# Stick-breaking attention: the logarithms as two fp32r halves for the triangle product

## The chip, the cores and the metric

The kernel runs on one core of a Trainium2 chip. The core has TensorE (matmul), VectorE, ScalarE, GpSimd and SyncE, each with its own instruction stream; streams meet only at semaphores. The metric is the device time of one execution in microseconds, as the median of several runs. "Rest", "values" and the other names of steps below are this document's.

## The reference

One inference step of a two-layer encoder for 512 prompt tokens and 64 sample tokens. Each layer has two feed-forward parts, a mixer with four branches, and a per-layer embedding. The change lies in the fourth branch, stick-breaking attention, with 4 heads of 64:

```python
z = jnp.einsum('bqhd,bkhd->bhqk', q, k).astype(jnp.float32) * (HEAD_DIM ** -0.5)
mask = k_pos[None, :] < q_pos[:, None]
log_beta = jax.nn.log_sigmoid(z)
log_1mb = jnp.where(mask, jax.nn.log_sigmoid(-z), 0.0)
rest = lax.cumsum(log_1mb, axis=3, reverse=True) - log_1mb
a = jnp.where(mask, jnp.exp(log_beta + rest), 0.0)
return jnp.einsum('bhqk,bkhd->bqhd', a.astype(v.dtype), v)
```

A key's weight depends on a sum of logarithms over all later keys up to the query. The kernel computes sp = log(1 + exp(z)), which is minus log_1mb, and z minus the sum of sp over the key itself and the later ones.

## The kernel before

All values are held transposed, features or keys on the 128 partitions and tokens along the free axis. Weights are split into a high part `whi` and a low part `wlo`, and activations into `u_hi` and `u_lo`, all of type fp32r; `products` (L587) multiplies three combinations of them in matmuls of 288 columns. GpSimd makes `wlo` (L1906), ScalarE `whi` (L554). The instruction order on each engine is written out by hand, and the stages follow each other.

The stick-breaking stage of a layer goes through 21 steps, listed in `SB` (L1417). For each of the 4 heads of the prompt there are four blocks of 128 keys, from the last block to the first. A block has the queries from its own position on, so it is 128, 256, 384 and 512 columns wide in this order. Then come five steps for the sample tokens, 256 columns each (4 heads by 64 queries): the 64 new keys and four blocks of cached keys. All prompt steps and the first sample step are diagonal: part of the block is masked.

A step i does this:

- TensorE, `sb_logits` (L1462, L1471): keys by queries, fp32, into PSUM bank 4 or 5.
- ScalarE (L1556 to L1558): absolute value, exp, log, into `sq`.
- VectorE (L1608): `spx` = max(z, 0) + that logarithm, and in a diagonal step the mask (L1576, L1575). The last of them raises `sb_sp`.
- TensorE, `sb_rest` (L1482): the triangle of minus ones `trineg` times `spx`, fp32, added to the logits in PSUM. In all but a head's first block L1486 adds minus the sum of the earlier blocks, kept in `sqsum`.
- VectorE, `finish` (L1584 to L1600): minimum with 0 into `arg`, the new `sqsum` (L1590, L1594, L1595), and after ScalarE's exp (L1563) the mask of `arg`.
- TensorE, `sb_values` (L1500, L1506): values by `arg`, into another bank.

TensorE's order in iteration i is logits(i), rest(i-1), values(i-2), and a quarter of one gate projection in fp32r (12 matmuls of L587, in the iterations 0 to 19). VectorE's order is finish(i-1), then spx(i). ScalarE does absolute value, exp and log of i, then the exp of i-1; after every fourth step it also copies the gate out of PSUM and rounds the next weight, after which GpSimd splits that weight.

Of the kernel before, what the change touches and what calls it, by code (L numbers as in the profile page):

```python
# [25 lines left out]
F32R = mybir.dt.float32r  # L26
ALU = mybir.AluOpType
# [5 lines left out]
T = SEQ + DEC  # L33
# [13 lines left out]
TB = (T + 127) // 128  # L47
# [6 lines left out]
F_, Q_, V_, G_, CA_, CB_, SQ_, SK_, SV_, BQ_, BK_, BV_ = 0, 2, 4, 6, 8, 10, 12, 14, 15, 16, 18, 20  # L54
NPROJ = 22
# [33 lines left out]
def trunk(nc, a, o):  # L89
# [3 lines left out]
    with ExitStack() as ctx:  # L93
        base = nc.sbuf_base
        arena = ctx.enter_context(nc.sbuf_tensor("arena", [128, (nc.sbuf_usable_end - base) // 4 - 16], F32))
        limit = nc.sbuf_usable_end
# [20 lines left out]
        keep = Region((base + 31) // 32 * 32)  # L117
# [6 lines left out]
        headones = keep("headones", [128])  # L124
        trineg = keep("trineg", [128])
        negones = keep("negones", [128])
        later = keep("later", [128])
        eye64 = keep("eye64", [CHUNK])
        lvmask = keep("lvmask", [6, CHUNK // 2])
# [40 lines left out]
        proj_at = rm.at  # L170
# [35 lines left out]
        sbtok = rb("sbtok", [TB, 512])  # L206
        spx = rb("spx", [2, 512])
        arg = rb("arg", [2, 512])


        gkeep = proj
# [29 lines left out]
        ps = ctx.enter_context(nc.psum_tensor("ps", [128, 8, 512], F32))  # L241
# [90 lines left out]
        sb_tok = sem("sb_tok")  # L332
# [3 lines left out]
        sb_sp = sem("sb_sp")  # L336
# [143 lines left out]
        def bounds_vector(dve):  # L480

            n = [0]

            def link(ins):
                n[0] += 1
                ins.then_inc(lb_step, 1)
                dve.wait_ge(lb_step, n[0])

            lg, mx, sm = lb_work[:, 0:4], lb_work[:, 4:6], lb_work[:, 6:8]
            link(dve.tensor_tensor(mx, lg[:, 0:2], lg[:, 2:4], ALU.max))  # L490
            link(dve.tensor_tensor(lg[:, 0:2], lg[:, 0:2], mx, ALU.subtract))
            link(dve.tensor_tensor(lg[:, 2:4], lg[:, 2:4], mx, ALU.subtract))
            for g in range(2):
                half = slice(64 * g, 64 * g + 64)
                link(dve.tensor_copy(sinkcol[half], sinks_all[half, :, :, g]))
            dve.wait_ge(lb_exp, 1)
            link(dve.tensor_tensor(sm, lg[:, 0:2], lg[:, 2:4], ALU.add))
            link(dve.reciprocal(sm, sm))
            link(dve.tensor_tensor(lg[:, 0:2], lg[:, 0:2], sm, ALU.mult))
            link(dve.tensor_tensor(lg[:, 2:4], lg[:, 2:4], sm, ALU.mult))  # L500
            link(dve.tensor_tensor(lb_all[:, 0, :], lg[:, 0:2], lg[:, 0:2], ALU.subtract))
            link(dve.tensor_tensor(lb_all[:, 1, :], lg[:, 0:2], lg[:, 2:4], ALU.add))
            link(dve.tensor_tensor(lb_all[:, 1, :], lb_all[:, 1, :], lg[:, 0:2], ALU.subtract))
            link(dve.tensor_scalar(lb1m[:], lb_all[:], -1.0, 1.0, ALU.mult, ALU.add))

        def setup_scalar(act):
            for n, name in enumerate(GAIN_NAMES):
# [16 lines left out]
        def layer(L):  # L524
# [6 lines left out]
            def before(s):  # L531

                return L * IN_LAYER[s]
# [226 lines left out]
            def link(dve, ins):  # L760

                steps[0] += 1
                ins.then_inc(dve_step, 1)
                dve.wait_ge(dve_step, steps[0])
# [661 lines left out]
            def sb_first(i):  # L1426
                return i == 0 or SB[i][0] != SB[i - 1][0]

            def sb_diagonal(i):

                hd, kb = SB[i]
                return hd is not None or kb is None
# [44 lines left out]
            def sb_rest(pe, i):  # L1477

                nk, w = sb_shape(i)
                bk = 4 + i % 2  # L1480
                pe.wait_ge(sb_sp, i + 1 + before(sb_sp))
                ins = pe.matmul(ps[0:nk, bk, 0:w], trineg[0:nk, 0:nk], spx[0:nk, i % 2, 0:w], start=False, stop=sb_first(i), skip_group_check=True)  # L1482
                if not sb_first(i):
                    q0, z0 = (0, 0) if SB[i][0] is None else (128 * SB[i][1] + 128, 128)
                    pe.wait_ge(sb_sum, sb_sums(i - 1) + before(sb_sum))
                    ins = pe.matmul(ps[:, bk, z0:w], negones[:], sqsum[:, q0:q0 + w - z0], start=False, stop=True, skip_group_check=True)  # L1486
                ins.then_inc(sb_arg, 1)
# [80 lines left out]
            def dve_sb(dve):  # L1568
                lk = lambda ins: link(dve, ins)

                def mask(i, x):

                    if SB[i][0] is None:
                        v = x[0:64, i % 2, 0:256].rearrange("p (h q) -> p h q", h=4)
                        return dve.tensor_tensor(v, v, later[0:64, 0:64].unsqueeze(1).to_broadcast([64, 4, 64]), ALU.mult)  # L1575
                    return dve.tensor_tensor(x[:, i % 2, 0:128], x[:, i % 2, 0:128], later[:], ALU.mult)  # L1576

                def finish(i):
                    hd, kb = SB[i]
                    nk, w = sb_shape(i)  # L1580
                    dve.wait_ge(sb_arg, i + 1 + before(sb_arg))
                    if i >= 2:
                        dve.wait_ge(sb_pv, i - 1 + before(sb_pv))
                    dve.tensor_scalar(arg[0:nk, i % 2, 0:w], ps[0:nk, 4 + i % 2, 0:w], 0.0, None, ALU.min).then_inc(sb_min, 1)  # L1584

                    if kb != 0:
                        if hd is None:
                            if kb is None:
                                lk(dve.memset(sqsum[:, 0:w], 0.0))
                            ins = dve.tensor_tensor(sqsum[0:nk, 0:w], sqsum[0:nk, 0:w], spx[0:nk, i % 2, 0:w], ALU.add)  # L1590
                        else:
                            q0 = 128 * kb
                            if not sb_first(i):
                                lk(dve.tensor_tensor(sqsum[:, q0 + 128:SEQ], sqsum[:, q0 + 128:SEQ], spx[:, i % 2, 128:w], ALU.add))  # L1594
                            ins = dve.tensor_copy(sqsum[:, q0:q0 + 128], spx[:, i % 2, 0:128])  # L1595
                        ins.then_inc(sb_sum, 1)
                        dve.wait_ge(sb_sum, sb_sums(i) + before(sb_sum))
                    if sb_diagonal(i):
                        dve.wait_ge(sb_exp, i + 1 + before(sb_exp))
                        mask(i, arg).then_inc(sb_a, 1)  # L1600

                for i in range(len(SB)):
                    nk, w = sb_shape(i)
                    z = ps[0:nk, 4 + i % 2, 0:w]
                    if i:
                        finish(i - 1)
                    dve.wait_ge(sb_ln, i + 1 + before(sb_ln))
                    ins = dve.scalar_tensor_tensor(out=spx[0:nk, i % 2, 0:w], in0=z, scalar=0.0, in1=sq[0:nk, i % 2, 0:w], op0=ALU.max, op1=ALU.add)  # L1608
                    if sb_diagonal(i):
                        lk(ins)  # L1610
                        ins = mask(i, spx)
                    ins.then_inc(sb_sp, 1)
                finish(len(SB) - 1)


# [480 lines left out]
```

## Time and profile before

| | us |
|---|---|
| median of 3 runs (3318.54 to 3319.71) | 3318.58 |
| the profiled execution | 3317.39 |
| its span, first to last instruction | 3315.7 |
| TensorE busy, 24147 matmuls | 3166.0 (95%) |
| VectorE busy | 1217.3 (37%) |
| ScalarE busy | 1101.5 (33%) |
| GpSimd busy | 1215.8 (37%) |
| share of TensorE in the chain that ended last | 87% |
| L1482, rest of the triangle: 32 records of 256 columns | 11.2, 431 ns each |
| stick-breaking stage, layer 0: first logits to last values | 788.0 to 880.9 |

The span is the time between the first and the last instruction; the execution's own time is 1.7 us more. An fp32 matmul leaves two records in the trace, an fp32r matmul one. The ends of matmuls are modelled, so a matmul's place is better read from its start and the start of the next one. "PEld" rows are weight loads.

### The profile page before, as it was taken

The numbers are of one execution on the slowest core, as the hardware profiler recorded it, in microseconds if no ns is written. First come the engines' busy times: TensorE is split into PE (matmuls) and PEld (weight loads), VectorE is DVE, ScalarE is ACT, GpSimd is POOL, SyncE is SP. The second block draws the span as 40 slices with busy tenths as digits, with TensorE's granted clock in tenths as the row PEclk, the third lists the DMA queues.
The fourth block names the chain that finished last, engine by engine and source line by source line (L and its number), as shares of the span: only waits on it lengthen the run. The fifth ranks groups of instructions, "written<-read, shape, count | busy, mean of one in ns | idle before, by whom it ended". The sixth has DMA issues, their size and how long they took to land.

```text
span 3315.7 us, 56545 instructions
## 1 busy us (share of the span) xinstructions
PE 3166.0 (95%) x24147; PEld 3037.2 (92%) x24147; DVE 1217.3 (37%) x1452; ACT 1101.5 (33%) x1528; POOL 1215.8 (37%) x564
## 2 busy tenths in 40 slices
PE   8999999899999999999989999998999999999998
PEld 7999989896799899999889999898867998999997
DVE  4232134744443423212342321348444434232124
ACT  3333222235433332322333332322354333323232
POOL 5433442231134433344343334423312344333443
PEclk9999999999999999999999999999999999999999
DMA  3222312221122122222112222122211221222221
GB/s 101 83 82 79 86 57 68 67 80 47 34 82 76 58 79 86 80 88 75 58 50 77 85 82 83 52 66 73 74 41 45 82 77 58 82 81 85 84 68 42
DMA packets 455951, 236.17 MB, mean 71 GB/s; under 512 B 18630, under 2 KB 454150, under 8 KB 455814
## 3 DMA queue, kind: packets, MB, share of 16 engines
q1 hardware_dynamic: 445792, 227.05, 23.5%
q10 hardware_dynamic: 10022, 7.15, 0.7%
q8 instruction: 104, 1.70, 0.2%
q14 instruction: 33, 0.27, 0.0%
HBM read 228.53 MB, written 5.63 MB: 71 GB/s over the span
## 4 chain that ended last, share of the span: by engine, by line
PE 87%; DVE 7%; ACT 3%; issue 1%; POOL 1%; ACTq 0%; DMA 0%; DVEq 0%; SPq 0%; POOLq 0%
PE ps L587 77%; PE ps L610 2%; PE ps L1482 1%; DVE uf L794 1%; PE ps L1781 1%; PE ps L620 1%; DVE sqsum L774 1%; PE ps L1500 1%; PE ps L1462 1%; DVE u_lo L788 1%; PE ps L604 1%; POOL u_lo L788 1%; DVE kgate L1094 0%; ACT u_hi L712 0%; PE ps L1486 0%
## 5 line engine op out<-in xcount | busy, mean ns | idle before, releaser
L1906 POOL TENSOR_TENSOR wlo<-wraw,whi 128x1024 fp32r<-128x1024 f32 x432 | 1078.3, 2496 | 1936.5 <-ACT whi L554 1936.0
L587 PE MATMUL ps<-u_hi,whi 128*128 128x288 f32 x4800 | 1055.1, 301 | 36.8 <-ACT ybr L1658 11.8
L587 PE MATMUL ps<-u_lo,whi 128*128 128x288 f32 x4800 | 1035.4, 297 | 0.0
L587 PE MATMUL ps<-u_hi,wlo 128*128 128x288 f32 x4800 | 1034.6, 297 | 0.0
L587 PEld LDWEIGHTS ps<-u_hi,whi 128*128 128x128 f32 x4800 | 770.0, 189 | 73.9 <-issue 31.6
L554 ACT ACTIVATE whi<-wraw 128x1024 fp32r<-128x1024 f32 x432 | 457.3, 1059 | 959.7 <-PE ps L587 959.3
L587 PEld LDWEIGHTS ps<-u_lo,whi 128*128 128x128 f32 x4800 | 773.5, 189 | 0.0
L587 PEld LDWEIGHTS ps<-u_hi,wlo 128*128 128x128 f32 x4800 | 773.4, 189 | 0.0
L837 DVE TENSOR_TENSOR sq<-sq,ps 128x576 f32<-128x576 f32 x88 | 66.4, 755 | 750.9 <-PE ps L587 750.9
L587 PE MATMUL ps<-s_hi,whi 128*128 128x288 f32 x1408 | 302.7, 296 | 0.0
L587 PE MATMUL ps<-s_lo,whi 128*128 128x288 f32 x1408 | 302.7, 296 | 0.0
L587 PE MATMUL ps<-s_hi,wlo 128*128 128x288 f32 x1408 | 302.7, 296 | 0.0
L774 DVE TENSOR_TENSOR sqsum<-sqsum,sq 128x576 f32<-128x576 f32 x70 | 102.5, 1465 | 506.7 <-ACT sq L689 505.2
L841 DVE TENSOR_TENSOR s_lo<-sq,s_hi 128x576 f32 x88 | 239.4, 2721 | 10.9
L587 PEld LDWEIGHTS ps<-s_lo,whi 128*128 128x128 f32 x1408 | 225.9, 188 | 0.0
L587 PEld LDWEIGHTS ps<-s_hi,whi 128*128 128x128 f32 x1408 | 225.8, 188 | 0.0
L587 PEld LDWEIGHTS ps<-s_hi,wlo 128*128 128x128 f32 x1408 | 225.5, 188 | 0.0
L1260 DVE SCALAR_TENSOR_TENSOR yc<-zc,taps_all,yc 128x606 f32<-128x606 f32 x120 | 142.6, 1189 | 4.2
L554 ACT ACT_TABLE_LOAD x44 | 56.5, 1283 | 229.7 <-PE ps L587 229.7
L788 POOL TENSOR_TENSOR u_lo<-uf,u_hi 128x576 fp32r<-128x576 f32 x40 | 60.3, 1515 | 80.7 <-ACT u_hi L712 79.8
L587 PE MATMUL ps<-m_split,whi 128*128 128x288 f32 x512 | 89.4, 297 | 0.3 <-DVE m_split L1690 0.3
L803 POOL TENSOR_TENSOR h<-h,uf 128x576 f32<-128x576 f32 x32 | 55.9, 1768 | 67.3 <-DVE uf L811 67.3
(273 smaller groups left out, 2639.0 us busy)
## 6 DMA issues: line engine op xcount, KB each, us to landing
wraw<-in_ffn_up SPq DMA_DIRECT2D x176, 512.0 KB, 3.7
wraw<-in_w_in SPq DMA_DIRECT2D x104, 512.0 KB, 3.7
wraw<-in_ffn_down SPq DMA_DIRECT2D x64, 512.0 KB, 4.0
wraw<-in_ffn_down SPq DMA_DIRECT2D x32, 384.0 KB, 3.3
wraw<-in_w_out SPq DMA_DIRECT2D x16, 512.0 KB, 3.8
wraw<-in_ple_gate_w SPq DMA_DIRECT2D x16, 512.0 KB, 3.9
wraw<-in_w_branch SPq DMA_DIRECT2D x16, 256.0 KB, 2.6
xtok<-in_x_prompt SPq DMA_DIRECT2D x4, 512.0 KB, 6.5
```

Of the source, the lines that this page charges most:

```text
L554: act.activation(whi[:, i % SPLIT, :], wraw[:, i % RAW, :], ACT.Copy).then_inc(w_rounded, 1)
L587: ins = pe.matmul(ps[:, 2 * p + f, 0:HT], wt[:, part, w], x[:, k, HT * f:HT * f + HT], start=start and n == 0 and c == 0, stop=stop and n ...
L604: pe.matmul(ps[:, 1, 0:128], ones[:], ident[:], start=True, stop=True)
L610: ins = pe.matmul(ps[:, 0, SAME * tb:SAME * tb + same], x[:, t0:t0 + 128], ones[:, 0:same], start=start and tb == 0, stop=stop and tb == T ...
L620: pe.matmul(flat(3)[:, 0:SEQ], ones[:], roots[:, 0:SEQ], start=True, stop=True)
L774: dve.tensor_tensor(sqsum[:], sqsum[:], sq[:, k % 2, :], ALU.add).then_inc(sq_added, 1)
L788: engine.tensor_tensor(u_lo[:, k, :], uf[:, k, :], u_hi[:, k, :], ALU.subtract).then_inc(signal, 1)
L803: engine.tensor_tensor(h[:, k, :], h[:, k, :], uf[:, k, :], ALU.add).then_inc(signal, 1)
L837: dve.tensor_tensor(halves(x), halves(x), pair(2 * q + 1), ALU.mult).then_inc(up_mul, 1)
L841: dve.tensor_tensor(s_lo[:, bass.ds(it * 2 + q, 1), :].rearrange("p a n -> p (a n)"), x, s_hi[:, bass.ds(it * 2 + q, 1), :].rearrange("p a ...
L1260: ins = dve.scalar_tensor_tensor(out=yc[:, c, :], in0=zc[:, c, w:w + YW], scalar=wc, in1=yc[:, c, :], op0=ALU.mult, op1=ALU.add)
L1906: pool.tensor_tensor(wlo[:, i % SPLIT, :], wraw[:, i % RAW, :], whi[:, i % SPLIT, :], ALU.subtract).then_inc(w_split, 1)
```

## The change

`spx` is split on VectorE in two halves of type fp32r: `spx_hi` is `spx` rounded, by a multiplication with 1, and `spx_lo` the remainder, by a subtraction. A copy of the triangle of type fp32r is made once. TensorE multiplies the triangle with the high half and then the low half, in place of one fp32 matmul. `sb_sp` is raised by the subtraction. The halves lie where the projected values and the cached keys were, which are no longer read by then. The product with `sqsum`, the logits and the values stay fp32.

```diff
@@ -124,6 +124,7 @@
         negones = keep("negones", [128])
+        trineg_r = keep("trineg_r", [128], F32R)
@@ -206,6 +207,11 @@
         arg = rb("arg", [2, 512])
+
+        rv = Region(proj_at + BV_ * T * 4)
+        spx_hi = rv("spx_hi", [2, 512], F32R)
+        assert rv.at <= proj_at + NPROJ * T * 4
+        spx_lo = Region(limit - 8192 - 32)("spx_lo", [2, 512], F32R)
@@ -502,6 +508,7 @@
             link(dve.tensor_scalar(lb1m[:], lb_all[:], -1.0, 1.0, ALU.mult, ALU.add))
+            link(dve.tensor_copy(trineg_r[:], trineg[:]))
@@ -1479,7 +1486,9 @@
                 pe.wait_ge(sb_sp, i + 1 + before(sb_sp))
-                ins = pe.matmul(ps[0:nk, bk, 0:w], trineg[0:nk, 0:nk], spx[0:nk, i % 2, 0:w], start=False, stop=sb_first(i), skip_group_check=True)
+                for x in (spx_hi, spx_lo):
+                    ins = pe.matmul(ps[0:nk, bk, 0:w], trineg_r[0:nk, 0:nk], x[0:nk, i % 2, 0:w], start=False, stop=sb_first(i) and x is spx_lo,
+                                    skip_group_check=True)
@@ -1606,10 +1615,13 @@
                     ins = dve.scalar_tensor_tensor(out=spx[0:nk, i % 2, 0:w], in0=z, scalar=0.0, in1=sq[0:nk, i % 2, 0:w], op0=ALU.max, op1=ALU.add)
+                    lk(ins)
                     if sb_diagonal(i):
-                        lk(ins)
-                        ins = mask(i, spx)
-                    ins.then_inc(sb_sp, 1)
+                        lk(mask(i, spx))
+                    if i == 0:
+                        dve.wait_ge(sb_tok, TB + 2 + before(sb_tok))
+                    lk(dve.tensor_scalar(spx_hi[0:nk, i % 2, 0:w], spx[0:nk, i % 2, 0:w], 1.0, None, ALU.mult))
+                    dve.tensor_tensor(spx_lo[0:nk, i % 2, 0:w], spx[0:nk, i % 2, 0:w], spx_hi[0:nk, i % 2, 0:w], ALU.subtract).then_inc(sb_sp, 1)
```


On VectorE, where the 512-column block of a head is followed by the next head's first block, before (`later` is the mask, `sb_ln` the wait for ScalarE's logarithm):

```order
L1608 SCALAR_TENSOR_TENSOR spx<-ps,sq 128x512 [waits sb_ln]
L1576 TENSOR_TENSOR spx<-spx,later 128x128 [waits dve_step]
L1584 TENSOR_SCALAR arg<-ps 128x512 [waits sb_pv,sb_arg]
L1576 TENSOR_TENSOR arg<-arg,later 128x128 [waits sb_exp]
L1608 SCALAR_TENSOR_TENSOR spx<-ps,sq 128x128 [waits sb_ln]
L1576 TENSOR_TENSOR spx<-spx,later 128x128 [waits dve_step]
```

And after, from the same place (lines are those of the changed file, 9 higher here):

```order
L1617 SCALAR_TENSOR_TENSOR spx<-ps,sq 128x512 [waits sb_ln]
L1585 TENSOR_TENSOR spx<-spx,later 128x128 [waits dve_step]
L1623 TENSOR_SCALAR spx_hi<-spx 128x512 [waits dve_step]
L1624 TENSOR_TENSOR spx_lo<-spx,spx_hi 128x512 [waits dve_step]
L1593 TENSOR_SCALAR arg<-ps 128x512 [waits sb_pv,sb_arg]
L1585 TENSOR_TENSOR arg<-arg,later 128x128 [waits sb_exp]
L1617 SCALAR_TENSOR_TENSOR spx<-ps,sq 128x128 [waits sb_ln]
L1585 TENSOR_TENSOR spx<-spx,later 128x128 [waits dve_step]
L1623 TENSOR_SCALAR spx_hi<-spx 128x128 [waits dve_step]
L1624 TENSOR_TENSOR spx_lo<-spx,spx_hi 128x128 [waits dve_step]
```

Two operations and their waits stand between the mask and the minimum; the signal for TensorE moved from the mask to the second of them.

On TensorE, the same step before: logits of the next head, rest, values, start of the next gate.

```order
L1462 MATMUL ps<-proj 128x128 [waits sb_min]
L1482 MATMUL ps<-spx,trineg 128x512 [waits sb_sp]
L1486 MATMUL ps<-sqsum,negones 128x384 [waits sb_sum]
L1500 MATMUL ps<-arg,sbtok 64x384 [waits sb_a]
L587 MATMUL ps<-u_hi,whi 128x288 [waits gate_out,w_split]
```

And after:

```order
L1469 MATMUL ps<-proj 128x128 [waits sb_min]
L1490 MATMUL ps<-spx_hi,trineg_r 128x512 [waits sb_sp]
L1490 MATMUL ps<-spx_lo,trineg_r 128x512
L1495 MATMUL ps<-sqsum,negones 128x384 [waits sb_sum]
L1509 MATMUL ps<-arg,sbtok 64x384 [waits sb_a]
L594 MATMUL ps<-u_hi,whi 128x288 [waits gate_out,w_split]
```

One fp32 matmul became two of fp32r; the wait for `sb_sp` stands ahead of the first.

## Rows read from the trace of the kernel before

**Rows 1.** Stretches of layer 0: from:to us, length, engines busy (instructions), granted clock.
```profile
803.00:820.00 17.00, 17.00 (x79) 10.80 (x78) 7.38 (x21) 9.39 (x19) 2.37 (x1) 1.00 0.11 32
...
884.00:886.00 2.00, 2.00 (x10) 2.00 (x10) 2.00 (x4) 2.00 (x4) 0.00 (x0) 0.50 0.00 0
```

**Rows 2.** Timeline, one head: start us, duration us, engine, line, operation, count.
```profile
810.81 0.29 DVE L1576 TENSOR_TENSOR spx<-spx,later 128x128 f32<-128x128 f32 x1
...
812.44 0.70 PE L1482 MATMUL ps<-spx,trineg 128*128 128x256 f32 x2
...
815.44 0.29 DVE L1576 TENSOR_TENSOR spx<-spx,later 128x128 f32<-128x128 f32 x1
...
815.45 1.12 PE L1462 MATMUL ps<-proj 64*128 64x512 f32 x2
...
816.50 0.91 PE L1482 MATMUL ps<-spx,trineg 128*128 128x384 f32 x2
...
817.25 0.59 PE L1486 MATMUL ps<-sqsum,negones 128*128 128x256 f32 x2
...
820.07 0.29 DVE L1576 TENSOR_TENSOR spx<-spx,later 128x128 f32<-128x128 f32 x1
...
820.57 1.13 PE L1482 MATMUL ps<-spx,trineg 128*128 128x512 f32 x2
...
821.53 0.81 PE L1486 MATMUL ps<-sqsum,negones 128*128 128x384 f32 x2
...
823.77 0.69 DVE L1576 TENSOR_TENSOR arg<-arg,later 128x128 f32<-128x128 f32 x1 [0.70 <-ACT arg L1563]
...
824.69 0.29 DVE L1576 TENSOR_TENSOR spx<-spx,later 128x128 f32<-128x128 f32 x1
...
825.47 0.49 PE L1482 MATMUL ps<-spx,trineg 128*128 128x128 f32 x2
...
825.88 1.07 PE L1500 MATMUL ps<-arg,sbtok 128*64 128x512 f32 x2
```

**Rows 3.** Timeline, fp32r matmuls of a gate part, TensorE.
```profile
814.56 0.43 PE L587 MATMUL ps<-u_hi,whi 128*128 128x288 f32 x2
...
814.82 0.43 PE L587 MATMUL ps<-u_lo,whi 128*128 128x288 f32 x2
```

**Rows 4.** Groups by line and shape, VectorE: busy us, mean ns, idle before.
```profile
L1594 DVE TENSOR_TENSOR sqsum<-sqsum,spx 128x256 f32<-128x256 f32 x8 | 3.3, 416 | 0.0
...
L1690 DVE TENSOR_TENSOR m_split<-msum,m_split 128x576 fp32r<-128x576 f32 x16 | 12.1, 758 | 0.5
...
L839 DVE TENSOR_SCALAR s_hi<-sq 128x576 f32 x88 | 40.8, 464 | 13.4 <-DVE sq L837 5.7
```

**Rows 5.** Timeline, first two steps of the stage, layer 0.
```profile
792.51 0.49 PE L1482 MATMUL ps<-spx,trineg 128*128 128x128 f32 x2 [1.60 <-DVE spx L1576]
...
794.44 0.29 DVE L1576 TENSOR_TENSOR spx<-spx,later 128x128 f32<-128x128 f32 x1
...
795.36 0.70 PE L1482 MATMUL ps<-spx,trineg 128*128 128x256 f32 x2
```

**Rows 6.** Timeline, last steps of the stage, layer 0.
```profile
876.01 1.60 DVE L1590 TENSOR_TENSOR sqsum<-sqsum,spx 128x256 f32<-128x256 f32 x1
...
877.65 0.42 DVE L1608 SCALAR_TENSOR_TENSOR spx<-ps,sq 128x256 f32<-128x256 f32 x1
...
878.13 0.70 PE L1482 MATMUL ps<-spx,trineg 128*128 128x256 f32 x2 [2.12 <-DVE spx L1608]
```

**Rows 7.** Timeline, where the sample group begins and one of its steps.
```profile
854.32 0.94 PE L1471 MATMUL ps<-proj 64*64 64x64 f32 x8
...
855.20 1.12 PE L1482 MATMUL ps<-spx,trineg 128*128 128x512 f32 x2
...
863.00 0.41 DVE L1608 SCALAR_TENSOR_TENSOR spx<-ps,sq 128x256 f32<-128x256 f32 x1
...
865.45 0.70 PE L1482 MATMUL ps<-spx,trineg 128*128 128x256 f32 x2
```

## The prediction, made before the changed kernel ran

> **What bounds the kernel now.** I read the table of stretches first, for the stage that the change touches: in a 17 us stretch of the stick-breaking stage TensorE is busy for all 17.00 us, VectorE for 7.38 [rows 1]. So TensorE looks like the bound and VectorE idle. Its matmul ends are modelled, though, so I went on to the timeline of one head, in order of time. I call the four pieces of a step i on TensorE logits (L1462, L1471), rest (L1482 and, after a head's first block, L1486), values (L1500, L1506) and gates (L587). rest(i) comes one step after logits(i), and it needs spx(i), VectorE's last product before it. The reader is to compare, for each rest, the end of VectorE's mask L1576 with the start of L1482 [rows 2]. From that end to TensorE's start the signal takes 0.06 us, as the one true wait shows (spx ends at 878.07, the rest starts at 878.13) [rows 6]. Then the slack of a step is:
> - 256 columns: ready 811.10, started 812.44, slack 1.28 us.
> - 384 columns: ready 815.73, started 816.50, slack 0.71.
> - 512 columns: ready 820.36, started 820.57, slack 0.15.
> - 128 columns: ready 824.98, started 825.47, slack 0.43.
>
> TensorE is the bound in the steady part, but with VectorE only 0.15 to 1.28 us behind it. TensorE waits for VectorE at two places of a layer: 1.60 us at the first rest [rows 5] and 2.12 us at the last [rows 6]. Both layers show the same pattern. What comes after the stage starts from its end, so what the stage gains or loses shifts the end of the kernel.
>
> **What the change takes off TensorE.** An fp32 rest of 384 columns takes 0.75 us to the next weight load (816.50 to 817.25), one of 512 takes 0.96 (820.57 to 821.53) [rows 2]: 1.64 ns a column and 0.12 fixed, four columns' time at 2.4 GHz. The fp32r matmuls of L587 follow each other at 0.26 us for two of 288 columns [rows 3]: 0.13 each, one column's time. Two such matmuls of w columns and the same fixed part make 0.56 us at 512, so 0.40 saved, 0.30 at 384, 0.20 at 256. At 128 the block is a head's first, its rest took 0.41 (825.47 to 825.88) [rows 2], and with weight loads that no longer hide well I count 0.10. A head saves 1.0 us. The sample group has five rests of 256 columns, 0.2 each. Bounds: nothing saved, if a switch between fp32 and fp32r costs what the passes give, and 1.07 a head, if exactly half of the four passes goes.
>
> **What it puts on VectorE, and on the path.** Each of the 21 steps of a layer gets two operations between the mask and the signal. The low half is a subtraction of two SBUF tensors: L1594 takes 0.416 us at 256 columns, L1690 0.758 at 576, with an fp32r result [rows 4]: 0.28, 0.42, 0.55 and 0.68 us for 128, 256, 384 and 512. The high half is the same operation as L839, 0.464 us at 576 [rows 4]; with about 0.15 fixed, like the subtraction, that is 0.22, 0.29, 0.36 and 0.43. Each waits for the one before through a semaphore, 0.03 us. Together 0.56, 0.77, 0.97 and 1.17 us. The upper bound for the high half is the subtraction's rate, 0.25 more at 512. Behind the signal VectorE's next operation is the minimum of the step, which waits for the rest anyway; behind the waiting L1482 on TensorE are L1486, values, gates and the next logits, so a late rest moves everything.
>
> Steady part, step by step, against the slacks above:
> - 256: 0.77 against 1.28, hidden; TensorE then is 0.2 early.
> - 384: 0.97 against 0.71 less 0.2, so TensorE waits 0.46. The rest is 0.3 shorter, TensorE is 0.16 late.
> - 512: slack 0.15 and 0.16; VectorE's chain runs through the minimum of the step before and is some 0.1 later (estimate). 1.17 + 0.1 - 0.31 = 0.96 of waiting; 0.4 shorter rest leaves 0.56.
> - 128: 0.56 against 0.43, 0.13 late by that count. But VectorE's mask L1576 at 823.77 took 0.69 us where others take 0.29, and now starts later, behind what held it. I take 0.
>
> A head: 0.46 + 0.96 - 1.0 = +0.42 us, four heads +1.68. The first head has more: its first rest already waited for VectorE, so 0.56 is added in full. In its second step the slack was 795.36 - 794.73 - 0.06 = 0.57 [rows 5]; VectorE is 0.56 later and TensorE 0.46, so 0.77 against 0.47, 0.30 late. Together +0.86. In the fourth head the logits that follow are the sample group's, 0.88 us up to the rest (854.32 to 855.20) where a head's first logits take about 0.42 [rows 7]; that hides 0.45 more. Sample group: spx is ready at 863.41, its rest starts at 865.45 [rows 7], so 0.77 is hidden and four rests save 0.8. The last rest waits for VectorE: +0.77 - 0.2 = +0.57. A layer: 1.68 + 0.86 - 0.45 - 0.8 + 0.57 = +1.86 us, two layers +3.7. The copy of the triangle to fp32r is one small VectorE operation in the first layer before its first wait for TensorE, where VectorE idles for microseconds: nothing. More semaphores and the shifted addresses: nothing.
>
> The profiled execution took 3317.4 us, 1.7 outside its span; the median of the runs shown is 1.2 above it. The difference is carried over to the median: 3318.6 + 3.7 = 3322.3.
>
> **The clock.** The granted clock is 1.00 in the stage and 0.50, the lower level of 1.2 GHz, from 884 to 886, with TensorE busy all the time [rows 1]; before that lay the wait of 2.12 us and the hand-over to the next stage. Here it costs while dense matmuls run. The change adds about 0.6 us of idle time before that place and moves it by 1.9 us, so more or less of the slow stretch can fall on dense matmuls: between -1.5 and +3.4 us a layer, of which I take 0. The Trainium skill ("TensorE: Matmul & The Clock Gate", HAM oscillation — how this bites in real kernels) says that idle gaps on TensorE bring the clock down and that it has to be earned again, which speaks against a change that adds waits. The trace agrees for the gap at the end of the stage; no row shows a fall from waits of about 1 us inside the stage, and by that rule alone the sum would be higher.
>
> **Rivals.**
> 1. *TensorE's gain wins.* If VectorE's two operations overlapped what is there (the mask's tail, slacks larger than the rows say), only the saving would count: 4 x 1.0 + 5 x 0.2 = 5 us a layer, 3308.6. For it: TensorE busy 17.00 of 17. Against it: slacks of 0.15 and 0.43 us, and a chain of semaphores that allows no overlap. The faster outcome also needs the first and last waits not to grow.
> 2. *VectorE becomes the bound outright.* The high half runs at the subtraction's rate (0.07 to 0.25 more a step) and the switches eat half of the saving. Per head the two late steps then cost 0.45 more and the saving is 0.5 less, the step of 128 comes 0.2 late: +1.1 a head. With 0.1 for the first steps and 0.4 more for five sample rests: +5 a layer, 10 in all, so 3332. It decides as soon as the two operations take over 1.3 us at 512 columns or the rest saves under 0.2. For it: the slack is gone at 512 even in the forecast. Against: L839 is the same kind of operation, to the same type, at 0.464.
> 3. *A slow clock after the stage.* The longer last wait lets the slow stretch fall on dense matmuls of the next stage: up to 3.4 us a layer beyond the forecast, 3325 to 3329.
> 4. *GpSimd holds up the new subtractions.* L1590, two SBUF inputs, took 1.60 us at 876.01 instead of about 0.42 [rows 6] while GpSimd split a weight. One such hit on a late step costs 1 to 2 us, four a layer 4 to 8. GpSimd's run comes at the same place in each head, so it would be all or none; the split of 512 starts well before it.
>
> **How the numbers follow.** About 0.2% (6.6 us) is what a measurement of this kernel can tell from no change. Forecast, +1 to +6.5 us: 0.60. Rival 1 in full or in part, below +1: 0.12, of which 0.05 lies beyond -6.6. Rivals 2, 3 and 4, above +6.5 us: 0.12, 0.08 and 0.05, and 0.03 for what I don't see. The range takes in both bounds of the two unknown costs and a slow stretch: 3316 to 3330. Faster by over 0.2% 0.05, within 0.2% 0.67, slower by over 0.2% 0.28.
>
> **What would show it.** Per head the stage lasts 17.5 us instead of 17.1; L1482's successors wait for the low half in the steps of 384 and 512 columns (about 0.5 and 1 us) and not in those of 256 and 128 after the first head; the last wait is some 0.8 us longer; two fp32r matmuls of 512 columns lie within 0.56 us of each other's successor. The high half at 0.43 us and the low at 0.68 for 512 columns. If rests of 384 and 512 start without a wait, or the high half takes 0.68, or an fp32r rest of 512 columns takes more than 0.75 us, the forecast's steps are wrong. So is its sum, if the time between the two stick-breaking stages changes.

## The result, and the profile after

| | before | after |
|---|---|---|
| median, 4 runs each (us) | 3318.56 (3317.40 to 3319.71) | 3341.64 (3340.34 to 3342.85) |
| profiled execution, its span (us) | 3317.39, 3315.7 | 3342.85, 3341.1 |
| mean granted clock of TensorE | 0.982 | 0.975 |
| stage, first logits to last values, layers 0 and 1 (us) | 92.97, 92.97 | 98.43, 95.54 |

The changed kernel is slower: ratio 1.0069 [1.0057, 1.0081], 23 us, where 3.7 were forecast and 3330 was the top of the range. The page of the changed kernel, its span, the busy time by engine and the shares of the chain that ended last:

```profile
span 3341.1 us, 56632 instructions
...
PE 3179.9 (95%) x24147; PEld 3052.8 (91%) x24147; DVE 1251.5 (37%) x1537; ACT 1101.9 (33%) x1528; POOL 1213.3 (36%) x564
...
PE 85%; DVE 9%; ACT 3%; issue 1%; POOL 1%; ACTq 0%; DMA 0%; DVEq 0%; SPq 0%; POOLq 0%
```

TensorE has as many records as before and is busy 14 us more, although the edit takes work off it. That is the first hint that its work ran slower somewhere. A head of the stage looks as forecast. The timeline of a head, the steps of 384 and 512 columns and the next head's first block (to be set against [rows 2]):

```profile
821.18 0.36 DVE L1623 TENSOR_SCALAR spx_hi<-spx 128x384 fp32r<-128x384 f32 x1
821.57 0.56 DVE L1624 TENSOR_TENSOR spx_lo<-spx,spx_hi 128x384 fp32r<-128x384 f32 x1
...
822.19 0.44 PE L1490 MATMUL ps<-spx_hi,trineg_r 128*128 128x384 f32 x1 [0.42 <-DVE spx_lo L1624]
...
822.64 0.59 PE L1495 MATMUL ps<-sqsum,negones 128*128 128x256 f32 x2
...
825.76 0.43 DVE L1623 TENSOR_SCALAR spx_hi<-spx 128x512 fp32r<-128x512 f32 x1
826.22 0.69 DVE L1624 TENSOR_TENSOR spx_lo<-spx,spx_hi 128x512 fp32r<-128x512 f32 x1
...
826.96 0.50 PE L1490 MATMUL ps<-spx_hi,trineg_r 128*128 128x512 f32 x1 [0.94 <-DVE spx_lo L1624]
...
827.54 0.81 PE L1495 MATMUL ps<-sqsum,negones 128*128 128x384 f32 x2
...
831.48 0.33 PE L1490 MATMUL ps<-spx_hi,trineg_r 128*128 128x128 f32 x1
```

TensorE now waits for the low half, 0.42 us at 384 columns and 0.94 at 512, and the rest of 512 columns takes 0.58 us to the next product (826.96 to 827.54) instead of 0.96. The first and the last rest of the stage, with the logits behind the first (to be set against [rows 5, 6]):

```profile
794.50 0.33 PE L1490 MATMUL ps<-spx_hi,trineg_r 128*128 128x128 f32 x1 [2.18 <-DVE spx_lo L1624]
...
796.85 1.65 PE L1469 MATMUL ps<-proj 64*128 64x384 f32 x2
...
884.60 0.47 PE L1490 MATMUL ps<-spx_hi,trineg_r 128*128 128x256 f32 x1 [3.10 <-DVE spx_lo L1624]
```

The second of these rows lasts 1.65 us, far over what its column count asks (512 columns take 1.12 in [rows 2]). A stretch right there has the granted clock at 0.50, the lower level of 1.2 GHz; before, it was at 1.00 from 743.5 to 880.0 us, of which [rows 1] show a part. The columns of such stretches are, from here on: from:to, length, busy us (count) of PE, PEld, DVE, ACT, POOL, granted clock, DMA share, GB/s.

```profile
797.00:799.00 2.00, 2.00 (x4) 0.92 (x5) 0.43 (x1) 0.46 (x1) 0.00 (x0) 0.50 0.00 0
```

Setting the two traces side by side, place by place, gives the lag of the changed kernel (start time after minus start time before):

| place | before, us | lag, us |
|---|---|---|
| stage of layer 0 begins | 788.0 | +1.4 |
| stage of layer 0 ends | 881.0 | +6.9 |
| token sums of the second feed-forward part's norm | 1109.7 | +8.5 |
| token sums ahead of the per-layer embedding | 1574.9 | +6.8 |
| feed-forward sums, layer 1 | 2118.8 | +13.6 |
| stage of layer 1 begins, ends | 2433.2, 2526.2 | +14.4, +16.9 |
| second feed-forward part's norm, layer 1 | 2755.0 | +18.7 |
| token sums ahead of the per-layer embedding, layer 1 | 3218.7 | +18.6 |
| end | 3315.7 | +25.4 |

The lag grows in the stages (5.5 and 2.6 us) and by 5 to 7 us each across the token sums ahead of the per-layer embedding, code that the change does not touch. These sums are 40 fp32 matmuls, 80 records in the trace. The stationary operand of each, the one that is loaded as weights, is a block of squares, and the moving one is 64 equal columns of ones, so that each sum is written 64 times over (L610, now L617). Before, the timeline row of the group and a stretch inside it:

```profile
1574.89 9.14 PE L610 MATMUL ps<-ones,sq 128*128 128x64 f32 x80 [0.74 <-ACT e L1806]
```
```profile
1575.00:1580.00 5.00, 5.00 (x46) 5.00 (x46) 0.00 (x0) 3.17 (x5) 2.35 (x1) 1.00 0.09 28
```

And after:

```profile
1581.73 14.86 PE L617 MATMUL ps<-ones,sq 128*128 128x64 f32 x80 [0.74 <-ACT e L1818]
```
```profile
1585.00:1590.00 5.00, 5.00 (x26) 5.00 (x25) 0.00 (x0) 1.37 (x2) 0.05 (x1) 0.50 0.38 105
1590.00:1595.00 5.00, 5.00 (x25) 5.00 (x25) 0.00 (x0) 1.37 (x2) 0.00 (x0) 0.50 0.01 3
```

The same 80 records take 14.86 us instead of 9.14, at a granted clock of 0.50 instead of 1.00: 26 records in 5 us instead of 46, TensorE busy all the time in both. The wait ahead of them is 0.74 us in both. Summed over the kernel, the stretches at 0.50 come to about 120 us before and 168 after. So the 23 us are, roughly, 8 in the two stages (2.6 each, and 2.9 more where the clock fell early in layer 0) and 11 or 12 in two groups of sums. Another 1.6 and 1.8 come between a stage's end and the next norm's sums, where the stretch at 0.50 lasts 10.2 us instead of 6.8 (880.0 to 886.8 before, 884.8 to 895.0 after, in layer 0).

### The profile page after: what moved, and what is told of

Its sections match the earlier page's. It is cut to its first block, busy times and chain, and to the rows that moved or that the text cites. A ratio compares the mean times of both kernels' runs of the same rounds, so it can differ in the third digit from the quotient of the medians.

```text
span 3341.1 us, 56632 instructions
## 1 busy us (share of the span) xinstructions
PE 3179.9 (95%) x24147; PEld 3052.8 (91%) x24147; DVE 1251.5 (37%) x1537; ACT 1101.9 (33%) x1528; POOL 1213.3 (36%) x564
## 4 chain that ended last, share of the span: by engine, by line
PE 85%; DVE 9%; ACT 3%; issue 1%; POOL 1%; ACTq 0%; DMA 0%; DVEq 0%; SPq 0%; POOLq 0%
PE ps L594 75%; PE ps L617 2%; DVE uf L801 1%; PE ps L627 1%; PE ps L1793 1%; DVE sqsum L781 1%; PE ps L611 1%; DVE u_lo L795 1%; PE ps L1490 1%; POOL u_lo L795 1%; DVE kgate L1101 0%; PE ps L1509 0%; DVE roots L1145 0%; ACT u_hi L719 0%; DVE roots L786 0%
## 5 line engine op out<-in xcount | busy, mean ns | idle before, releaser
L611 PE MATMUL ps<-ident,ones 128*128 128x128 f32 x528 | 84.7, 324 | 1.6 <-DVE lb_work L483 1.6
```

Of the source, the lines that this page charges most:

```text
L611: pe.matmul(ps[:, 1, 0:128], ones[:], ident[:], start=True, stop=True)
```

## The experiments

Two theories stood against each other. P: the stage costs 2 to 3 us a layer, and the rest comes from when later work is reached, since the clock is granted or not at another place. W: the time is the work and the waits that the change adds. Each kernel was timed beside the kernel before in three rounds; ratios are to that. "Spare matmuls" are fp32 products of `ones` and `ident`, 128 columns, into a PSUM bank that is free there; nobody reads the result. The kernel before has such matmuls of its own around its norms (`keep_clock`, L604).

**shift_before** is the kernel before, without the split, with 12 spare matmuls behind each stage.

```diff
+                for _ in range(12):
+                    pe.matmul(ps[:, 3, 0:128], ones[:], ident[:], start=True, stop=True)
```

> The kernel before with nothing of the change, but 12 more fp32 matmuls of 128 columns on TensorE at the end of each stick-breaking stage (0.21 us each, 2.6 us a layer, no idle time added). Theory P (place in time: most of the 23 us comes from stretches at the lower clock, mainly in the normalisation ahead of the per-layer embedding, which appear or not depending on when that place is reached): the total does not rise by the 5.1 us of added work but differs from that by over 3 us, and the difference sits in stretches at clock 0.50 outside the stick-breaking stages. Theory W (work: the change's own instructions cost it all, wherever they are): 3318.6 + 5.1 = 3323.7, within 1.5 us, and the other stages as long as before.

3326.84 us (3325.52 to 3327.75), ratio 1.0023 [1.0014, 1.0033]: 7.5 us for 5.1 of added work. In layer 0 the sums are long here too, in layer 1 not:

```profile
1573.72 14.95 PE L610 MATMUL ps<-ones,sq 128*128 128x64 f32 x80 [0.74 <-ACT e L1808]
```

So spare work alone, without the change, brought slow sums about. It did so without a delay: they are reached at 1573.72 us, 1.2 earlier than before, since the stretch at 0.50 behind the stage is 3.4 us long instead of 6.8. The total says less: it departs from the 5.1 us of added work by 2.4, under the 3 that theory P expected, and the interval (4.6 to 11 us) holds 5.1 as well.

**shift_after** is the changed kernel with 8 spare matmuls behind each stage, 1.7 us a layer.

> The changed kernel with 8 more fp32 matmuls of 128 columns on TensorE at the end of each stick-breaking stage (1.7 us a layer). Theory P: the total changes by something other than +3.4 us, down as well as up; if the normalisation ahead of the per-layer embedding escapes the lower clock in one layer, about 5 us come back, 3341.6 + 3.4 - 5 = 3340 or less. Theory W: 3345.0 within 1.5 us.

3326.12 us (3325.05 to 3328.14), ratio 1.0021 [1.0011, 1.0031]. The changed kernel with 3.4 us of useless work added is 15.5 us faster than without. The row of the sums and a stretch in them:

```profile
1578.47 9.14 PE L617 MATMUL ps<-ones,sq 128*128 128x64 f32 x80 [0.74 <-ACT e L1820]
```
```profile
1583.00:1588.00 5.00, 5.00 (x47) 5.00 (x47) 0.00 (x0) 2.32 (x4) 0.00 (x0) 1.00 0.35 105
```

Both groups of sums are short again, at a clock of 1.00, though both stages now have the fall inside them (98.43 and 98.36 us). More work took less time, as P has it and W cannot. The two groups of sums give back 11.5 us. A smaller part lies right behind the stages: the stretch at 0.50 there lasts 6.8 us in both layers instead of 10.2. The spare matmuls stand where TensorE was partly idle, so their effect is more than a delay: the sums of layer 0 are reached 3.3 us earlier than in the changed kernel.

**dve_only** makes both halves on VectorE but leaves the rest an fp32 product with the unsplit `spx`.

```diff
-                for x in (spx_hi, spx_lo):
-                    ins = pe.matmul(ps[0:nk, bk, 0:w], trineg_r[0:nk, 0:nk], x[0:nk, i % 2, 0:w], start=False, stop=sb_first(i) and x is spx_lo,
-                                    skip_group_check=True)
+                ins = pe.matmul(ps[0:nk, bk, 0:w], trineg[0:nk, 0:nk], spx[0:nk, i % 2, 0:w], start=False, stop=sb_first(i), skip_group_check=True)
```

> Only VectorE's part of the change: both halves are made and the signal comes after the low half, but TensorE multiplies the unsplit spx in one fp32 matmul as before. By the slacks, a head then costs 0.26 + 0.02 us at 384 columns and about 1.0 to 1.2 us at 512, 0 to 0.1 at 128, so a head's period is 18.3 to 18.5 us instead of 17.1 (the changed kernel: 17.64), and the stage 6 to 8 us longer than before. Theory P expects the total beside that to move by several us in either direction at clock 0.50; theory W expects 3318.6 + 12 to 16 = 3331 to 3335 and no difference elsewhere.

3347.07 us (3337.83 to 3349.05), ratio 1.0077 [1.0060, 1.0094]. A head takes 18.38 us, 1.3 more than before and 0.74 more than after; the stages take 99.98 us. The waits in one head:

```profile
825.03 1.13 PE L1489 MATMUL ps<-spx,trineg 128*128 128x512 f32 x2 [0.93 <-DVE spx_lo L1622]
...
838.34 0.91 PE L1489 MATMUL ps<-spx,trineg 128*128 128x384 f32 x2 [0.22 <-DVE spx_lo L1622]
```

VectorE's two operations alone cost a head what was expected (a period of 18.3 to 18.5 us). The total is 12 us above the upper end of theory W. The sums are long again in both layers.

**pe_only** makes `spx` itself fp32r and lets both matmuls read it, so no halves are made: the low half is left out and the high one counted twice. The main lines, against the changed kernel:

```diff
-        spx = rb("spx", [2, 512])
+        spx = rb("spx", [2, 512], F32R)
...
-                for x in (spx_hi, spx_lo):
+                for n_, x in enumerate((spx, spx)):
...
-                    lk(dve.tensor_scalar(spx_hi[0:nk, i % 2, 0:w], spx[0:nk, i % 2, 0:w], 1.0, None, ALU.mult))
-                    dve.tensor_tensor(spx_lo[0:nk, i % 2, 0:w], spx[0:nk, i % 2, 0:w], spx_hi[0:nk, i % 2, 0:w], ALU.subtract).then_inc(sb_sp, 1)
...
+                    ins.then_inc(sb_sp, 1)
```

> Only TensorE's part: spx is written by VectorE's existing operations as fp32r, no high and low half are made, and both fp32r matmuls read the same tile (so the low half is left out of the computation and the high half counted twice). No step waits for VectorE longer than before, so a head is 1.0 us shorter (period 16.1 us) and the stage about 4.5 to 5 us shorter. Theory W: 3318.6 - 9 to 10 = 3309. Theory P: the stage gains the same, but the total departs from 3309 by over 3 us, at clock 0.50 outside the stage.

3324.49 us (3313.62 to 3325.96), ratio 1.0013 [1.0003, 1.0023]. A head takes 16.29 us (822.73 to 839.02 in the rows) and the stages 89.2, 3.75 less than before in each layer, where 4.5 to 5 were expected. The rest of 512 columns starts 0.06 us behind the end of VectorE's mask, so it waits for VectorE even here, by a little (0.58 us from the logits to it, 0.42 before):

```profile
822.73 0.70 PE L1469 MATMUL ps<-proj 64*128 64x256 f32 x2
...
834.55 0.48 PE L1469 MATMUL ps<-proj 64*128 64x128 f32 x2
...
834.78 0.29 DVE L1585 TENSOR_TENSOR spx<-spx,later 128x128 fp32r<-128x128 f32 x1
...
835.13 0.73 PE L1490 MATMUL ps<-spx,trineg_r 128*128 128x512 f32 x2
835.70 0.81 PE L1495 MATMUL ps<-sqsum,negones 128*128 128x384 f32 x2
...
839.02 0.70 PE L1469 MATMUL ps<-proj 64*128 64x256 f32 x2
...
1569.67 14.99 PE L617 MATMUL ps<-ones,sq 128*128 128x64 f32 x80 [0.74 <-ACT e L1815]
```

The stages are 7.5 us shorter together, and the kernel is slower than before. The last row says why: the sums are reached at 1569.67 and run slowly (in layer 1 too). Rival 1's saving is real at 0.8 us a head, and was lost to the clock. One of this kernel's ten runs took 3313.62, with a mean granted clock of 0.980 where the others had 0.976 or 0.977.

**The sums at 96 columns.** The number of equal columns of ones, `SAME`, is free. Made 96 instead of 64, it adds TensorE columns to these sums and changes nothing else. Two kernels, the changed one and the one before, have this edit:

```diff
-            SAME = 64
+            SAME = 96
```

> The changed kernel, but the token sums of the normalisations of h (80 matmul records each, 6 such places) use 96 instead of 64 columns of the ones; a record takes 0.11 us there either way if the weight load is what paces it. Theory P (the clock falls in the sums ahead of the per-layer embedding at some arrival times because TensorE does too little in them): at full clock each place still takes 9 us, the two that took 14.5 us take 9, and the total falls by 10 us or more, to 3331 or less. Theory W: the sums take longer or as long, nothing else moves, 3341.6 or more.

3326.78 us (3325.34 to 3327.87), ratio 1.0021 [1.0012, 1.0031], 14.9 us less than the changed kernel.

```profile
1579.61 9.17 PE L617 MATMUL ps<-ones,sq 128*128 128x96 f32 x80 [0.74 <-ACT e L1818]
```

> The kernel before with the same 96 columns. Its sums already ran at the full clock. Theory P: no long fall appears, 3318.6 within 4 us, and the changed kernel with 96 columns stands 5 to 8 us above it, which is what the two stages cost by themselves. Theory W: the difference between the two stays 23 us.

3317.48 us (3315.78 to 3319.44), ratio 0.9998 [0.9988, 1.0007]. The kernel before, whose sums were short, gains nothing. A record of 96 columns takes the 0.11 us of one of 64, so no work was saved: what went away is the slow stretch. With it gone from both, the change costs 9.3 us, more than the 5 to 8 expected, of which 7.9 lie in the stages (98.42 and 95.36 against 92.96 and 92.97).

A rival is that the 96 columns only moved the arrival (1579.61 instead of 1581.73). The kept traces speak against it, if the arrival is counted from the end of the last stretch at 0.50 ahead of the sums:

```profile
1564.00:1567.00 3.00, 2.75 (x8) 1.54 (x7) 1.01 (x2) 0.11 (x1) 0.00 (x0) 0.50 0.38 114
...
1568.00:1584.00 16.00, 14.96 (x114) 14.51 (x113) 9.13 (x12) 8.82 (x13) 11.22 (x6) 1.00 0.12 34
```

These two are of the changed kernel, whose stretch at 0.50 ends at 1567.4 us, 14.3 ahead of its sums. The kernels with 64 columns have twelve such groups. Seven began 14.32 to 14.63 us behind that end, and all seven were long; the fall came 2.4 to 2.8 us after their first matmul. Five began 12.22 to 14.23 us behind it, and all five were short. Of the sixteen groups with 96 columns four began 14.32 to 14.48 us behind it, where every group of 64 was long, and all were short. The border is narrow (14.23 against 14.32) and was found in the traces afterwards; no run was made to test it.

**sums96_after_shift** adds the 8 spare matmuls a layer of shift_after to sums96_after.

> The changed kernel with 96 columns and with the 8 extra matmuls at the end of each stage (3.4 us) that took 15.5 us off the changed kernel. Theory P: with the sums out of the clock's reach the arrival time matters little, and this costs what it adds: sums96_after plus 3.4, within 3 us. If the 96 columns have no part in it, this run is again about 15 us faster than sums96_after.

3326.22 us (3324.74 to 3328.20), ratio 1.0021 [1.0012, 1.0031], 0.6 below sums96_after. The spare work that took 15.5 us off now takes off next to nothing, so most of its effect had gone through the sums. But its 3.4 us of work do not show either (3327.2 to 3333.2 was expected), and the stage of layer 1 has its clock fall again (98.35 against 95.36). What pays for both lies behind the stages: from a stage's end to the next norm's sums this kernel takes 2.1 and 2.4 us less than sums96_after although 1.7 us of work stand in between, and the stretch at 0.50 there is 6.8 us long instead of 10.2.

**sums96_values_first** is sums96_after with something for TensorE to do while the low half is made: values(i-2) goes ahead of rest(i-1).

```diff
-                    if 0 <= i - 1 < len(SB):
-                        sb_rest(pe, i - 1)
                     if i >= 2:
                         sb_values(pe, i - 2)
+                    if 0 <= i - 1 < len(SB):
+                        sb_rest(pe, i - 1)
```

> The changed kernel with 96 columns, and with the values of step i-2 ahead of the rest of step i-1 on TensorE. The values (0.31 to 1.0 us) need nothing that is late there, so they fill the waits of 0.42 us at 384 and 0.94 us at 512 columns. A head's period falls from 17.64 to 16.4 to 16.8 us, the stage from 95.5 to 91 to 93 us, the total to 6 to 9 us below sums96_after. If VectorE's chain paces the steps instead (the rest delayed by the values delays the minimum, and that the next spx), the period stays at 17.4 us or more.

3323.73 us (3322.03 to 3324.76), ratio 1.0009 [0.9998, 1.0019]. A head takes 16.50 us instead of 17.64, the stages 91.30 and 94.23, but only 3.05 us less arrive at the end, where 6 to 9 were expected. The wait at 384 columns is gone, the one at 512 stays:

```profile
834.27 0.44 PE L1490 MATMUL ps<-spx_hi,trineg_r 128*128 128x384 f32 x1
...
836.83 0.48 PE L1469 MATMUL ps<-proj 64*128 64x128 f32 x2
837.25 0.86 PE L1509 MATMUL ps<-arg,sbtok 128*64 128x384 f32 x2
...
839.03 0.50 PE L1490 MATMUL ps<-spx_hi,trineg_r 128*128 128x512 f32 x1 [0.93 <-DVE spx_lo L1624]
```

Where the gain went, in two stretches at the end of the stage and behind it:

```profile
874.00:880.00 6.00, 2.83 (x20) 1.92 (x20) 3.17 (x6) 0.98 (x3) 1.33 (x1) 0.56 0.29 89
880.00:886.00 6.00, 3.30 (x17) 3.14 (x16) 4.66 (x7) 4.97 (x9) 0.00 (x0) 0.50 0.00 0
```

TensorE was busy for less than half of the six microseconds ahead of 880, and a stretch at 0.50 of 13.7 us (874.7 to 888.4) lay there in each layer.

**Cover for the idle places.** The last four kernels all have the sums at 96 columns and put spare matmuls where TensorE waited. The three numbers given for each are those ahead of the first rest, ahead of the last rest, and behind the stage. The lines that place them:

```diff
+                        spare(pe, {0: 9, len(SB) - 1: 13}.get(i - 1, 0))
                         sb_rest(pe, i - 1)
                     pe_gate_part(pe, GATES_SW, 2 * KD, i, QUARTERS)
+                spare(pe, 12)
```

**busy_values_first** is sums96_values_first with this (9, 13, 12).

> sums96_values_first with 34 spare fp32 matmuls of 128 columns a layer where TensorE sits idle: 9 ahead of the first rest, 13 ahead of the last, 12 behind the stage, while the next stage's inputs are made. Theory P: with the idle time covered the clock stays at 1.00 in the stage and after it, the 13.7 us at clock 0.50 behind each stage and the 6.8 us in layer 1's first head go, and the total falls from 3323.7 to 3308 to 3315, below the kernel before. If waits don't bring the clock down, it stays at 3323.7 or rises by what the spare matmuls delay.

3305.89 us (3305.30 to 3312.18), ratio 0.9968 [0.9955, 0.9980]. This beats both kernels, by 12.9 us the one before (3318.77 beside it) and by 35.8 the changed one. The page's span, the cover at the first rest, and the two stretches of above:

```profile
span 3303.8 us, 56904 instructions
```
```profile
789.51 2.27 PE L1521 MATMUL ps<-ident,ones 128*128 128x128 f32 x18
```
```profile
874.00:880.00 6.00, 5.04 (x48) 4.57 (x47) 1.70 (x5) 2.15 (x5) 0.00 (x0) 1.00 0.32 91
880.00:886.00 6.00, 6.00 (x48) 6.00 (x48) 4.69 (x8) 3.24 (x6) 0.00 (x0) 1.00 0.00 0
```

In layer 0 the clock stays at 1.00 from 743 to 1550 us. The stretches at 0.50 add up to 86 us, where the same order without the cover (sums96_values_first) has 151 and takes 17.8 us longer. The stages take 91.50 us each.

**busy_before** is the cover alone on the kernel before (7, 9, 12), without the split.

> The kernel before with 96 columns in the sums and the same cover (7, 9 and 12 spare matmuls). It says whether the change has any part in a gain: theory P expects 3312 to 3317, and busy_values_first 1 to 4 us below this, from a head of 16.5 instead of 17.1 us and a last wait 0.8 us longer.

3313.69 us (3312.44 to 3314.73), ratio 0.9985 [0.9976, 0.9995], stages 92.7 us, 103 us at 0.50. So of the 12.9 us that busy_values_first gains, about 5 come from cover and sums, and 7.8, more than the 1 to 4 expected, from the split with the values ahead: 2.4 by shorter stages, and the rest goes with 17 us less at 0.50. No run has the values ahead without the split, so it is not shown that the split is needed for this; what speaks for it is that the steady part of the kernel before has no wait to fill.

**busy_after** is the same with the changed kernel's own order (9, 13, 12).

> The changed kernel in its own order, with 96 columns and the same cover. Theory P: the stage takes 95.0 to 95.6 us in both layers, without the clock's fall that made it 98.4 in layer 0, and the total is that of busy_before plus 2 x 2.0 to 2.6 us. If the change costs more than its stages by itself, it is above that.

3313.65 us (3312.33 to 3322.05), ratio 0.9985 [0.9976, 0.9995]. The stages take 94.75 and 94.78 us, without a fall of the clock, 2.0 more than in busy_before; the whole kernel takes the same. Two of its ten runs took 3321.5 to 3322.05. The total was expected 4 to 5 us above busy_before. The clock gives the 4 us back: the eight short runs have a mean granted clock of 0.987, the ten of busy_before 0.984 or 0.985, which by an estimate from these means is 86 us at 0.50 instead of about 103. At which place is not settled, since the profiled execution is one of the two long ones (0.982 and 0.983).

**busy_pe_only** is pe_only with the cover (7, 9, 12) and the 96 columns; the low half is left out as there.

> pe_only (no halves made on VectorE, both fp32r matmuls read the same tile, so the low half is left out) with 96 columns and the cover of 7, 9 and 12. The stage is 3.7 us shorter than before, as in pe_only. Theory P: the total is busy_before less 7.5, within 3 us. Theory W, by which pe_only's 3324.5 was work: above busy_before.

3303.58 us (3302.23 to 3306.52), ratio 0.9952 [0.9936, 0.9969]: 10.1 below busy_before, within the 3 us around 7.5 that were expected, with stages 4.5 shorter each. With the sums and the idle places out of the way, a shorter stage does arrive at the end, which it did not in pe_only.

## Why the prediction was wrong

The step that failed is the clock: "between -1.5 and +3.4 us a layer, of which I take 0". It came to some 9 us a layer (23 less 4 to 5 for the stages' own cost, over two). It was placed only behind the stage, with one stretch there [rows 1] to read it from; that stretch lasts 6.8 us in the kernel before (880.0 to 886.8), and half of it is the 3.4. It came mostly from two other places: the token sums 700 us later (5.7 and 5.8 us in the two layers) and, in layer 0, the stage itself (2.9). That a few microseconds of spare work move the time by more than themselves is shown by shift_after, that they bring slow sums about without the change by shift_before, and that the larger part goes through the sums by sums96_after. "What the stage gains or loses shifts the end of the kernel" fails with it: pe_only's stages gave 7.5 us, and the kernel took 5 more. Rival 3, a slow clock, had the right cause with the wrong place and about a third of the size. The last sentence of the prediction named the sign by which its sum would fail, the time between the two stages changing, and that is what happened: the lag grew by 7.5 us there.

The rest, step by step:

- *Saving on TensorE, 0.40, 0.30, 0.20 and 0.10 us at 512, 384, 256 and 128 columns.* Measured from start to next product: 0.58 against 0.96, 0.45 against 0.75, 0.34 against 0.53, 0.37 against 0.41. Right, but for 0.04 instead of 0.10 at 128. A switch between fp32 and fp32r cost nothing that shows.
- *VectorE's two operations, 0.43 and 0.68 us at 512.* These rows have all of that width in the changed kernel:

```profile
L1624 DVE TENSOR_TENSOR spx_lo<-spx,spx_hi 128x512 fp32r<-128x512 f32 x8 | 5.5, 692 | 0.3
...
L1623 DVE TENSOR_SCALAR spx_hi<-spx 128x512 fp32r<-128x512 f32 x8 | 3.4, 426 | 0.3
```

  Right to 0.01 us at every width (227 and 293 ns at 128, 294 and 426 at 256, 359 and 559 at 384). The Trainium skill ("VectorE: DVE Perf Modes", The perf-mode tier table) gives a multiplication by a scalar in fp32 from SBUF twice the rate of an operation on two tensors. The trace agrees: from 128 to 512 columns the one grows by 199 ns and the other by 399. Rival 2, which had both at one rate, falls with it.
- *Waits of 0.46 and 0.96 us in a head.* 0.42 and 0.94. Right. None at 256 columns after the first head.
- *A head +0.42.* 17.64 against 17.09 us: +0.55. The 0.06 less saved at 128 columns explains half of the difference.
- *First head +0.42 and +0.86.* +1.23 in layer 1 (18.77 against 17.54). Right.
- *Fourth head and sample group, -0.26 together.* +0.22 (layer 1's 2.57 less 1.23, 0.55 and 0.57), but this is the clock again. The rests of the last two steps start 0.79 us farther apart (4.41 against 3.62), as forecast; the wait itself grew by 0.98 (3.10 against 2.12), since TensorE reached it 0.2 earlier. Then, in both layers, the clock fell right at the last rest (2540.2 in layer 1):

```profile
2539.97 0.39 PE L1490 MATMUL ps<-spx_hi,trineg_r 128*128 128x256 f32 x1 [3.10 <-DVE spx_lo L1624]
...
2540.37 1.05 PE L1495 MATMUL ps<-sqsum,negones 128*128 128x256 f32 x2
```

  The matmul behind it takes 1.05 us where the same shape takes 0.59 at full clock. With the clock held, busy_after against busy_before, this part comes to -0.28.
- *A layer +1.86.* +2.05 with the clock held (94.75 against 92.7), +2.57 in layer 1 of the changed kernel. The sum without the clock was right to 0.2 us a layer.
- *Rival 1, TensorE's gain wins.* pe_only shows the gain alone at 0.8 us a head, dve_only the cost alone at 1.3. The forecast had 1.0 for the gain; the waits eat it, as forecast. *Rival 4, GpSimd holds the subtraction.* None of the 42 subtractions took over 0.70 us.

The chances were wrong as well: the case that came had no chance of its own, since no rival let the clock fall far from the stage.

The profile before held a warning. [Rows 1] show a stretch with TensorE busy for 2.00 of 2 us at 0.50, and such stretches add up to 120 us over the kernel, which the forecast did not count. The experiments show that a change of arrival can move such stretches. The Trainium skill ("TensorE: Matmul & The Clock Gate", What's actually happening) says that the monitor behind the clock runs on its own time and does not begin anew with a kernel's work. No run here shows the monitor itself; that one and the same kernel has two levels of time agrees with it (below). The Trainium skill ("TensorE: Matmul & The Clock Gate", HAM oscillation — how this bites in real kernels) puts the falls down to idle gaps. That fits the stretches behind the stage, which the cover removed, and not the sums, where TensorE was busy for 5.00 of 5 us and the same wait of 0.74 us stood ahead of the short and of the long ones.

What stays open: where the lag of 1.4 us ahead of the stage of layer 0 comes from, where busy_after wins back its 4 us, and why the clock falls in 64-column sums and not in those of 96. Arrival counted from the kernel's start does not tell when it falls: in layer 1 the 64-column sums were long at 3218.3 (pe_only) and short at 3218.7 (before). Counted from the end of the last slow stretch it does, in all twelve groups (14.5 and 14.2 us for these two), but that is a pattern and not a reason.

## What to carry to other kernels

Before the effect of a change of a few microseconds is forecast in a kernel that TensorE bounds, add up its time at the lower clock from the rows of granted clock; if it is many times the change's price, the forecast's range must cover a good part of it, wherever it lies. To tell a change's own price from arrival, add a little spare work to both kernels, and compare the touched stage by itself. Moving two VectorE operations onto a signal that TensorE waits for paid here only with independent TensorE work ahead of the wait: with the idle places covered in each, the split cost 2.0 us a stage in its own order and saved 1.2 with the values ahead.

## What the runs showed of the hardware

- The same 40 fp32 matmuls of 64 columns (80 records) took 9.1 or 14.9 to 15.1 us, at a granted clock of 1.00 or mostly 0.50 (layer 0: short when reached at 1574.89 and 1578.47, long at 1569.67, 1573.72, 1581.73 and 1582.35). They were long in all seven cases that began 14.32 us or more behind the end of the last slow stretch, and in none of the five that began 14.23 or less behind it. A record of 96 columns took no longer than one of 64 (0.11 us), and its group took 9.2 us in both layers of all eight kernels that had it, reached from 1568.2 to 1579.9 and from 3206.7 to 3228.8.
- One kernel can have two levels of time, and the shorter runs had the higher mean granted clock: pe_only 3313.6 (one run, 0.980) and about 3324.5 (0.976), dve_only 3337.8 (one run, 0.979) and about 3347 (0.975), busy_after about 3313.5 (0.987) and two at 3321.8 (0.983), busy_values_first about 3305.5 (0.987) and two at 3312 (0.984).
- 3.4 us of useless matmuls took 15.5 us off a kernel of 3341.6.
- Waits of 0.42 and 0.94 us in each head did not lower the clock; behind the stage's first wait, 2.18 us in layer 0 and 2.19 in layer 1 of the same run, it was at 0.50 in layer 0 and stayed at 1.00 in layer 1. In the kernels with this wait and no cover the clock fell there in 7 of 12 stages; with the 1.6 us of the kernel before it fell in none of 8, and with spare matmuls in the wait in none of 8.
